# A two-layer decoder step in fp32: rotary positions by transfers between partitions instead of a matrix product, and a rearranged order of the small work

## What is computed

```python
def layer(x, l, pos, mem_k, mem_v, past_k, past_v):
    x = x + 0.5 * swiglu(rms_norm(x, ffn1_norm[l]), ffn1_w1[l], ffn1_w3[l], ffn1_w2[l])
    mixed, k_new, v_new, sgu_v = token_mixing(rms_norm(x, mix_norm[l]), pos, mem_k, mem_v, past_k, past_v, ...)
    x = x + mixed
    x = x + 0.5 * swiglu(rms_norm(x, ffn2_norm[l]), ffn2_w1[l], ffn2_w3[l], ffn2_w2[l])

def token_mixing(xn, pos, mem_k, mem_v, past_k, past_v, w_in, ...):
    a_u, a_v, b_q, b_k, b_v, c_q, gates = split(xn @ w_in)
    y_a = gelu(a_u) * chunk_spatial_gate(layer_norm(gelu(a_v)), s_w, s_b)
    q, k, v = rope(b_q, pos), rope(b_k, pos), b_v          # 8 heads of 64
    y_b = moba_attention(q, pos, k_all, v_all)             # block-sparse; past pages for sampled tokens
    y_c = cross_attention(c_q, mem_k, mem_v)               # 4 heads of 128
    g_a, g_b, g_c = split(sigmoid(gates))
    merged = g_a * (y_a @ w_a) + g_b * (y_b @ w_b) + g_c * (y_c @ w_c)
    return merged @ w_o, k, v, v_n

def rope(x, pos):                                          # halves of 32 in a head of 64
    return concatenate([x1 * cos - x2 * sin, x2 * cos + x1 * sin], axis=-1)
```

## Time and profile before

| | us |
|---|---|
| median of 3 runs | 1539.08 (1538.97 to 1541.28) |
| profiled execution, its own time | 1539.5 |
| its span | 1537.8 |
| PE busy | 1511.5 (98 %) |
| DVE busy | 897.2 (58 %) |
| ACT busy | 704.0 (46 %) |
| POOL busy | 84.8 (6 %) |

### The profile page before, as it was taken

The page is one execution under the profiler, slowest core; times in us unless marked ns, Lnnn a source line. Parts: engine busy times, 40 slices in busy tenths (PEclk is TensorE's granted clock), DMA queues, the critical chain, the costliest instruction groups (busy, mean ns, idle before and its releaser), DMA issues.

```text
span 1537.8 us, 29029 instructions
## 1 busy us (share of the span) xinstructions
PE 1511.5 (98%) x12196; PEld 1455.0 (95%) x12196; DVE 897.2 (58%) x1219; ACT 704.0 (46%) x928; POOL 84.8 (6%) x164
## 2 busy tenths in 40 slices
PE   8999999999999999999999999999999999999997
PEld 8999999998887999999999999999988879999996
DVE  6766456565644675554565654664666447755544
ACT  6444335355633454443454443533665425544432
POOL 0000000230012000000000000003100210000000
PEclk9999999999999999999999999999999999999998
DMA  6455658695498444455545466669855965444552
GB/s 257 165 178 189 189 179 307 243 366 167 162 318 318 152 159 164 166 164 162 168 162 177 167 199 184 228 239 322 301 179 180 348 226 179 165 165 165 159 165 79
DMA packets 106002, 313.74 MB, mean 204 GB/s; under 512 B 12880, under 2 KB 12880, under 8 KB 105744
## 3 DMA queue, kind: packets, MB, share of 16 engines
q1 hardware_dynamic: 94320, 273.74, 53.2%
q0 software_dynamic: 11552, 38.15, 6.7%
HBM read 306.07 MB, written 5.77 MB: 203 GB/s over the span
## 4 chain that ended last, share of the span: by engine, by line
PE 95%; DVE 3%; ACT 1%; issue 1%; DMA 0%; SPq 0%; DVEq 0%; ACTq 0%
PE res L471 82%; PE gb L553 2%; PE gb L562 2%; PE res L493 1%; PE gb L532 1%; DVE wlo L1166 1%; PE gb L747 1%; PE gb L755 1%; PE gb L545 1%; PE gb L569 0%; DMA wraw<-in_ffn_w 0%; PE gb L723 0%; PE gb L726 0%; PE gb L505 0%; PE gb L688 0%
## 5 line engine op out<-in xcount | busy, mean ns | idle before, releaser
L1166 DVE TENSOR_TENSOR wlo<-wraw,whi 128x1024 fp32r<-128x1024 f32 (+2 forms) x448 | 512.3, 1148 | 528.7 <-ACT whi L867 527.6
L471 PE MATMUL res<-norm_hi,whi 128*128 128x288 f32 x2176 | 654.9, 301 | 8.5 <-ACT gate_sigmoid L878 3.8
L867 ACT ACTIVATE whi<-wraw 128x1024 fp32r<-128x1024 f32 (+2 forms) x448 | 443.4, 994 | 458.1 <-PE res L471 391.6
L471 PE MATMUL res<-norm_lo,whi 128*128 128x288 f32 x2176 | 642.5, 295 | 0.0
L471 PE MATMUL res<-norm_hi,wlo 128*128 128x288 f32 x2176 | 640.7, 294 | 0.0
L471 PEld LDWEIGHTS res<-norm_hi,whi 128*128 128x128 f32 x2176 | 408.5, 188 | 21.2 <-issue 7.5
L471 PEld LDWEIGHTS res<-norm_lo,whi 128*128 128x128 f32 x2176 | 409.4, 188 | 1.3
L471 PEld LDWEIGHTS res<-norm_hi,wlo 128*128 128x128 f32 x2176 | 410.3, 189 | 0.0
L471 PE MATMUL res<-h_hi,whi 128*128 128x288 f32 x1024 | 305.1, 298 | 0.8 <-DVE h_lo L1608 0.7
L471 PE MATMUL res<-h_lo,whi 128*128 128x288 f32 x1024 | 302.1, 295 | 0.0
L471 PE MATMUL res<-h_hi,wlo 128*128 128x288 f32 x1024 | 301.4, 294 | 0.0
(11 more groups left out here) (218 smaller groups left out, 1110.1 us busy)
## 6 DMA issues: line engine op xcount, KB each, us to landing
wraw<-in_ffn_w SPq DMA_DIRECT2D x240, 512.0 KB, 3.5
wraw<-in_w_in SPq DMA_DIRECT2D x96, 512.0 KB, 5.5
wraw<-in_ffn_w SPq DMA_DIRECT2D x32, 384.0 KB, 3.3
page_Q<-in_cache_k POOLq DMA_DIRECT2D x48, 256.0 KB, 6.5
page_Q<-in_cache_k SPq DMA_DIRECT2D x40, 256.0 KB, 5.5
page_Q<-in_cache_v SPq DMA_DIRECT2D x40, 256.0 KB, 5.6
wraw<-in_w_mem_kv SPq DMA_DIRECT2D x16, 512.0 KB, 3.5
page_Q<-in_cache_v POOLq DMA_DIRECT2D x32, 256.0 KB, 6.7
```

Of the source, the lines that this page charges most:

```text
L471: mm = pe.matmul(res[:, 2 * s + c, 0:n], w_, m_, start=begin and k == 0 and j == 0, stop=end and k == kh - 1 and j == 2)
L867: act.activation(whi[n % NH][:, 0:kh, :], wraw[n % NR][:, 0:kh, :], ACT.Copy).then_inc(hi_done, 1)
L1166: dve.tensor_tensor(wlo[n % NR][:, 0:kh, :], wraw[n % NR][:, 0:kh, :], whi[n % NH][:, 0:kh, :].bitcast(F32), ALU.subtract).then_inc(lo_don ...
```

## The change

**Rotation.** The products and the swap matrix go. Behind the evacuation of each two tiles of q or k, POOL issues four transfers from work to qk, each of which brings 32 partitions to the place of their neighbours. The sign is in the table of sines. DVE multiplies the shifted rows by it and the rows themselves by cos, in operations of 1152 elements. ACT waits with the evacuation of v, which reuses work, until q is rotated (rope_q). All 16 key quads stand in fours behind halves 11, 15, 19 and 23, those of the memory at step 4.

```diff
-QUAD_STEP = {Q_MK + i: 2 + 2 * (i // 2) for i in range(4)}
+QUAD_STEP = {Q_MK + i: 4 for i in range(4)}
...
 def quad_unit(q):
-    return U_SLOT + (q | 1) if q < Q_MK else step_unit(QUAD_STEP[q] + 1) - 1
+    return U_SLOT + (q | 3) if q < Q_MK else step_unit(QUAD_STEP[q] + 1) - 1
...
-            w_in_half(4)
-            w_in_half(5)
-            pe.wait_ge(evac[0], RES * L + RES_FFN + RES_MEM + 1)
-            rotate(L, "q", 0)
-            rotate(L, "q", 1)
...
-            w_in_half(11)
-            keys(2)
-            keys(3)
+            for i in range(4, 12):
+                w_in_half(i)
+            for i in range(0, 4):
+                keys(i)
...
-            keys(4)
-            keys(5)
...
-            keys(6)
-            keys(7)
+            for i in range(4, 8):
+                keys(i)
```

```diff
+            sinb = cst[:, C_SIN:C_SIN + T].unsqueeze(1).broadcast_to([P, 4, T])
+
+            def rope_sin(o, shifted):
+                dve.wait_ge(shifted, 128 * (L + 1))
+                step(dve.tensor_tensor(qk[:, o:o + 4, :], qk[:, o:o + 4, :], sinb, ALU.mult))
+
+            def rope_cos(o, done_):
+                step(dve.tensor_tensor(work[:, o:o + 4, :], work[:, o:o + 4, :], cosb, ALU.mult))
+                dve.tensor_tensor(qk[:, o:o + 4, :], qk[:, o:o + 4, :], work[:, o:o + 4, :], ALU.add).then_inc(done_, 1)
+                dve.wait_ge(done_, L + 1)
...
-            step(dve.tensor_tensor(qk[:, 0:4, :], work[:, 0:4, :], cosb, ALU.mult))
             lo(q + 8)
             lo(q + 9)
-            rotate("q", 0)
+            rope_sin(0, q_shifted)
             lo(q + 10)
-            rotate("q", 2)
+            rope_cos(0, rope_q)
...
-            if L:
-                dve.wait_ge(out_k, 16 * L)
-            step(dve.tensor_tensor(qk[:, 4:8, :], work[:, 4:8, :], cosb, ALU.mult))
             slot(0)
-            rotate("k", 0)
             slot(1)
+            rope_sin(4, k_shifted)
             slot(2)
-            rotate("k", 2)
-            dve.sem_inc(rope_k, 1)
+            rope_cos(4, rope_k)
...
+            act.wait_ge(rope_q, L + 1)
             take(v + 1, 0, work[:, 0:2, :], ACT.Copy)
...
+            for t in range(4):
+                pool.wait_ge(evac[t % 2], r + RES_MEM + 1 + t // 2)
+                if t == 2 and L:
+                    pool.wait_ge(out_k, 16 * L)
+                for b in range(4):
+                    pool.dma_start(qk[32 * b:32 * b + 32, 2 * t:2 * t + 2, :],
+                                   work[32 * (b ^ 1):32 * (b ^ 1) + 32, 2 * t:2 * t + 2, :])\
+                        .then_inc(q_shifted if t < 2 else k_shifted, 16)
```

```diff
+    def own_heads(name):
+
+        at_ = 512 * banks[name][0]
+        diagonal = gb[:].rearrange("p b f -> p (b f)")[:, at_:at_ + 4 * 136].rearrange("p (c x) -> p c x", x=136)
+        return diagonal[:, :, 0:P].rearrange("p c (b r) -> p c b r", r=32)
...
+        def turned_rows(name, rows_):
+            transposes(name, [rows_[:, c * P:(c + 1) * P] for c in range(4)],
+                       [bk(name)[:, c * P:(c + 1) * P] for c in range(4)])
...
+                if n in (12, 13):
+                    i = n - 12
+                    drained(f"mo{i}.{L}")
+                    turned_rows(f"moT{i}.{L}", S[:, 0, 512 * (1 - i):512 * (2 - i)])
...
-                    claim(f"oT0.{L}")
                     drained(f"oG0.{L}")
-                    own_heads(f"oT0.{L}", 0, S[:, 0, 0:512]).then_inc(filled_of(f"oT0.{L}"), 1)
+                    turned_rows(f"oT0.{L}", S[:, 0, 0:512])
                 if n == 29:
-                    claim(f"oT1.{L}")
                     drained(f"oG1.{L}")
-                    own_heads(f"oT1.{L}", 0, S[:, 1, 0:512]).then_inc(filled_of(f"oT1.{L}"), 1)
+                    turned_rows(f"oT1.{L}", S[:, 1, 0:512])
...
-                o4 = bk(nm)[:, 0:P].rearrange("p (c b r) -> p c b r", b=4, c=4)
+                o4 = own_heads(nm)
```

```diff
 
 
...
-                if n < HEADS:
-                    head_scores(n)
+                if n == 0:
+                    head_scores(0)
...
-                if 1 <= n <= HEADS:
-                    head_turn(n - 1)
-                if n in (2, 4):
...
+                if n + 1 < HEADS:
+                    head_scores(n + 1)
+                if 1 <= n <= HEADS:
+                    head_turn(n - 1)
...
+                if 3 <= n <= HEADS + 2 and (n - 3 >= 8 or n % 2 == 0):
+                    m = n - 3
+                    nm = f"O{m - m % 2}.{L}" if m < 8 else f"O{m}.{L}"
+                    wait(fill(nm))
+                    if m < 8:
+                        dve.tensor_copy(qk[0:HD, m // 2, 0:SEQ], bk(nm)[0:HD, 0:SEQ])
+                        dve.tensor_copy(qk[HD:P, m // 2, 0:SEQ], bk(nm)[HD:P, SEQ:2 * SEQ]).then_inc(emptied_of(nm), 1)
+                    else:
+                        dve.tensor_copy(cq[:, m - 8, 0:SEQ], bk(nm)[:, 0:SEQ]).then_inc(emptied_of(nm), 1)
```

```diff
-                to = acc[:, 2 * g:2 * g + 2, :]
-                dve.tensor_tensor(to, to, scaled[:], ALU.add).then_inc(m_f, 1)
                 lo(u0 + 2 * g + 4)
                 if g:
                     merged_low(g - 1)
+                to = acc[:, 2 * g:2 * g + 2, :]
+                dve.tensor_tensor(to, to, scaled[:], ALU.add).then_inc(m_f, 1)
                 lo(u0 + 2 * g + 5)
...
+                    if g >= 2:
+                        stage = 3 * L + (1 if f == 1 else 3)
+                        add_squares(stage, g - 1, 2 if stage == 3 * DEPTH else 3)
                     add_to_x(u + 1, g, g % 2, 0.5)
                     if gain is not None:
                         low(2 * g, F + 1, gain)
                         low(2 * g + 1, F + 1, gain)
-                    if g >= 2:
-                        stage = 3 * L + (1 if f == 1 else 3)
-                        add_squares(stage, g - 1, 2 if stage == 3 * DEPTH else 3)
```

```diff
-            pe.wait_ge(lo_done, i + 1)
+            if i:
+                pe.wait_ge(lo_done, i + 1)
             order = [(c, k) for k in range(kh) for c in range(2)] if ready else [(c, k) for c in range(2) for k in range(kh)]
             for c, k in order:
+                if i == 0 and c == 0 and k % 2 == 0:
+                    pe.wait_ge(*((lo_done, 1) if k else (first_lo, 1)))
...
-        pe.wait_ge(ones_ready, 1)
-        for _ in range(16):
-            pe.matmul(gb[:, 3, 0:P], ones, ones, start=True, stop=True)
...
+            if n == 0:
+                act.activation(whi[0][:, 0:2, :], wraw[0][:, 0:2, :], ACT.Copy).then_inc(first_hi, 1)
+                act.activation(whi[0][:, 2:4, :], wraw[0][:, 2:4, :], ACT.Copy).then_inc(hi_done, 1)
+                return
...
-            if g == 0:
-                square(0)
...
         hi(2)
-        for g in range(1, 4):
+        for g in range(4):
             square(g)
...
-                if F == 0 and i == 1:
+                if F == 0 and i == 3:
                     dve.wait_ge(memsq_ready, 1)
...
-        sp.dma_start(gains[:], A["gains"]).then_inc(ld_gain, 16)
         for g in range(4):
             sp.dma_start(x[:, 2 * g:2 * g + 2, :], A["x_T"][:, 2 * g:2 * g + 2, :]).then_inc(ld_x[g], 16)
+            if g == 0:
+                sp.dma_start(gains[:], A["gains"]).then_inc(ld_gain, 16)
...
+                if L == 0 and n == 10:
+                    sp.dma_start(memn[:], A["mem_T"]).then_inc(ld_mem, 16)
+                if L == 0 and n == 14:
+                    sp.dma_start(cst[:], A["const"]).then_inc(ld_const, 16)
```

```diff
-        pe.wait_ge(sq_ready, 4 * (3 * DEPTH + 1))
         for k in (6, 7):
+            pe.wait_ge(sq_ready, 4 * 3 * DEPTH + k - 2)
             mm = pe.matmul(bk("rsf")[:, 0:T], ones, work[:, k, :], start=False, stop=k == 7)
...
+        def last_x(g, s):
+
+            if g == 3:
+                act.activation(stat[:, 95:96], epsc, ACT.Sqrt)
+            act.wait_ge(x_ready, 4 * (3 * DEPTH - 1) + g + 1)
+            if g == 3:
+                act.activation(work[:, 6, :], x[:, 6, :], ACT.Square, scale=D ** -0.5).then_inc(sq_ready, 1)
+            taken(s)
+            if g == 3:
+                act.activation(work[:, 7, :], x[:, 7, :], ACT.Square, scale=D ** -0.5).then_inc(sq_ready, 1)
+                return
+            square(g)
+            final_gain(2 * g)
+            final_gain(2 * g + 1)
+
+        def final_gain(k):
+            act.activation(yout[:, k, :], x[:, k, :], ACT.Copy, scale=gains[:, G_FINAL + k:G_FINAL + k + 1])\
+                .then_inc(xg_ready, 1)
...
-        act.activation(stat[:, 95:96], epsc, ACT.Sqrt)
+        final_gain(6)
         deviation("rsf")
+        final_gain(7)
...
-        for g in range(4):
-            for k in (2 * g, 2 * g + 1):
-                i = dve.scalar_tensor_tensor(yout[:, k, :], x[:, k, :], gains[:, G_FINAL + k:G_FINAL + k + 1],
-                                             rstd[:], ALU.mult, ALU.mult)
-            i.then_inc(nf_ready, 1)
+        for g in (0, 1, 3):
+            dve.wait_ge(xg_ready, 2 * g + 2)
```

(6 more changed lines are left out.)

173 lines of the change are left out of this document (64 added, 109 removed).

## The result

The changed kernel took 1528.46 us in the median of four runs (1527.0 to 1529.07), the kernel before 1539.73 (1538.97 to 1541.28): a ratio of 0.9926 (95 % interval 0.991 to 0.9941), 11.3 us faster where 24.5 were forecast. The profiled execution of after took 1527.0, with a span of 1525.3: 12.5 less than the one of before.

The account below looks back on a forecast made before the run. The prediction took PE as the bound, with 95 % of the span's chain on it. Terms of 28.1 us off and 3.6 on gave −24.5, from 1539.08 to 1514.6 us, range 1508.5 to 1521.5.

Parts of the forecast that it names:

- turned heads: Turning of heads, memory heads included: transposes replace products with the identity on PE, 3.5 us less in both layers.
- transposes last: Some 11 steps: weight products restart faster behind transposes (0.21) than behind fp32 scores (0.32), 2.2 us less in both layers.
- copies of O: PE's waits for DVE's copies of O go, since the copies now precede softmax; 6.5 us less with ramps.
- c3: PE's wait for scaled at small unit c3 goes, as it now stands where DVE has slack; 2.1 us less.
- ends of FFNs: At FFN ends the sum of squares goes ahead of x, its inputs being there; no cost.
- (a): Before the transposes of past probabilities behind half 16, PE waits 0.8 for the exponential; 1.6 us more in both.
- (b): Step 1 to 2 of the gates: PE waits 0.5 longer for ACT's sigmoid; 1.0 us more.
- clock (c): Behind the sigmoid wait, a fall of PE's granted clock gets likelier in layer 0; 0.7 us more, half a fall.
- end: Behind the last x: reciprocal 2.4 sooner, three products on DVE with POOL doing the fourth 1.4 less; taken as −3.5.
- rival 2: At the end DVE and POOL share a port, losing about 1.2 of the 1.4; 1515.8 us, chance 0.10.
- Rival 1: Late probabilities replace the waits for O's copies, so the 6.5 stay; 1521 us, chance 0.14.
- Rival 3: Rotation's shifted rows land late and PE starves at half 10 or 11; 1545 us at 25 us landing, chance 0.03.

Follow-up runs that it names:

- e_ffn: The changed kernel with the sums of squares at the ends of FFNs, the last included, behind the new x again; 1528.02 us in one run.
- e_ydve: The changed kernel with all four products of the end on DVE and no arithmetic on POOL; 1522.25 us, ratio to before 0.988.
- e_turn: The changed kernel with the transposes back at the front of the small work of a step; 1523.94 us in one run.
- e_mot: The changed kernel with the second turn of memory heads in small bank 1 in place of bank 0; 1523.92 us.
- b_pt0: The kernel before, with ACT copying the transposes of head 0 behind the sigmoid of step 2; 1534.01 us, ratio 0.9963.
- e_pt0: The changed kernel with all end products on DVE, transposes in front, and ACT's copy of head 0's transposes behind step 2's sigmoid; 1512.17 us, ratio 0.982.
- best2: e_pt0 plus products of ones, old orders at FFN ends and w_b's tiles, memory turn in bank 1, past-probability transposes one half later; 1511.64 us.
- best3: e_pt0 with the old order at all FFN ends but the last, products of ones, and first square of x ahead of the first weights; 1510.3 us.
- b_rot: The kernel before with the rotation by transfers alone, everything else unchanged; 1532.36 us, ratio 0.9945.

## Why the prediction was wrong, point by point

The terms in us for both layers, as the profiles of before and after show them at their places:

| term | forecast | measured |
|---|---|---|
| rotation | −7.6 | −7.6 |
| quads in fours | −2.3 | −2.6 |
| turned heads | −3.5 | −3.5 |
| transposes last | −2.2 | 0 |
| copies of O | −6.5 | −6.6 |
| c3 | −2.1 | −2.0 |
| start | −0.4 | −0.5 |
| ends of FFNs | 0 | +0.9 |
| new wait (a), past probabilities | +1.6 | +1.8 |
| new wait (b), sigmoid | +1.0 | +1.3 |
| step 2, low parts of y_a | – | +1.1 |
| bank of the second memory turn | – | +1.4 |
| w_b | +0.3 | +0.35 |
| clock (c) | +0.7 | 0 in the profile |
| end | −3.5 | +3.8 |
| sum | −24.5 | −12.2 (spans: −12.5) |

**The end** is the step that failed, by 7.3 of the 12. Its first half, −2.4 to the reciprocal, was measured at −2.2; but 1.9 of this hang on the order of the sums at the last FFN end (e_ffn), the edit that the prediction priced at nothing under the FFN ends, and not on taking the squares apart. The second half, three products on DVE at 0.7 and the fourth on POOL "meanwhile", missed two things. The port: DVE's second product took 1.95 against 0.76 for the first, and the three 3.29, not 2.1 (DVE's products; ns min/median/max, changed kernel, then e_ydve, where POOL has none):

```profile
L1635 DVE TENSOR_TENSOR y_out<-y_out,rstd x3: 744/758/1950, 1513.3 to 1515.8; 128x576 f32<-128x576 f32 x3
```

```profile
L1635 DVE TENSOR_TENSOR y_out<-y_out,rstd x4: 750/752/758, 1515.5 to 1517.5; 128x576 f32<-128x576 f32 x4
```

This was rival 2, and so far it gave its 1.2. The Trainium skill, SBUF — State Buffer, section "Who interferes with whom", says that DVE and GpSimd share a pair of ports to SBUF, and that the one that issues first holds the pair for the whole instruction. The trace agrees: POOL's product takes 1.90, of which 0.64 lie under DVE's first, and DVE's second ends 0.6 behind POOL's, one product of its own. And what I had not in any rival: POOL's drain of 10 us, which sets the end 5.4 behind where the stores would have (−2.2 to the reciprocal, −0.2 in the products, +0.8 in the stores, three of which are now issued in a row behind the late products, +5.4: +3.8). The prediction asked which engine is done first, and never what an engine does after its last instruction. The row was to be had: before's trace has the drain too, but no view shows it as work, and at 1247 it waited for nobody.

**Transposes last.** The 0.10 of faster restart was read from two rows behind different blocks. I priced one side of a change of form and took the other side as free; in e_turn the same 0.1 stands behind the scores, in the changed kernel ahead of the transposes. With its waits the reorder costs 3.3 us, so it was a loss, as e_turn showed; in the table these stand under (b), under step 2 and in the bank's 1.4, of which 1.0 go also when the transposes move back.

**Nothing new from quads and memory turns.** I had looked for who needs the results of a moved step. For the second memory turn I missed who holds its bank (e_mot). For step 2 I missed a chain through ACT.

**Ends of FFNs.** "Its inputs are there: nothing" was right for the inputs and wrong for the queue: the sum of 0.75 us stands ahead of the last x, and the sum of squares behind it is waited for.

**The clock.** I took half a fall more. The profiled run had as many as before; the median of the changed kernel, 1528.46, lies 1.5 above its profiled run, which would be one fall more than in that run. Of those other three runs only the mean granted clock is on record: 0.994, 0.994 and 0.996, against 0.995 in the profiled one. Two of them fit one fall more, the one of 1528.56 us with 0.996 doesn't, so this stays open. The term was of the right kind: every one of these falls lies behind a wait that the change made longer, and none is seen once one copy has moved (b_pt0, e_pt0, best2, best3).

**What held.** The forecast's large terms, rotation, copies of O, turned heads and c3, came within 0.1 each, and both new waits foreseen, (a) and (b), came where and as long as said. Rival 1 (the wait for O's copies replaced by others) did not happen as a replacement. Rival 3 had the transfers late beyond 22 us; they land 3.7 after issue in the median, 5.9 at most in layer 0. In size, the range had room for waits moving but not for a whole mechanism at the end: the end's gain was bounded by 2.5 and 4.5 us, and a loss wasn't excluded by any row, only by the habit of counting engines that compute.

## What to carry over

Before giving an idle engine work at the very end, look when its program ends now: its own ending may take longer than the work, and is hidden only while it comes early. A faster restart behind one kind of product may be paid back on the other side of the block, as here, so price both sides before moving its parts. And where a wait of 2 us stands in a saturated kernel, ask what stands ahead in the queue of the engine waited for: one copy moved behind the sigmoid was worth 5.1 us here, 1.5 of them in clock.

## What the runs showed of the hardware

- POOL's drain at the end of its program took 9.3 to 11.4 us in the eight traces where no arithmetic stands ahead of it (10.04 before, 9.93 in e_ydve, 9.70 behind a mere wait, 9.27 in b_pt0, 11.35 in b_rot), and 11.29 in the changed kernel with 1.56 of its product in it. What it does in this time no run shows.
- POOL's product of 576 elements took 1.90 beside DVE, 1.26 if it stood still for the 0.64 that lie under DVE's first product. By the figure in the Trainium skill, GPSIMD Engine Reference, section "Elementwise — side-by-side cycle accounting", my estimate was 1.3; with that reading the trace agrees. No run has the product alone.
- Transfers between partitions, four of 32 partitions for each two tiles, 72 KB each, landed in 2.0 to 5.9 us after issue in layer 0; the issue took 0.5 us of POOL.
- Between the first units and the last, the clock fell only behind the longest wait, for 3.41 us each time, in some executions and not in others with the same wait of 1.9 to 2.5 us; without that wait, or with 0.4 of it, in none of four profiles.
